# Weight row, output chunks and a third place for the last unit's turned banks: a hand-planned hybrid attention layer

## The reference, cut to what matters

```
h = rmsnorm(x, norm_g)
q, k, v, g of groups A, B, C, and f_logit = split(h @ w_in)      # w_in: 1024 x 6152
A: stick-breaking attention  w[t,s] = sigmoid(z[t,s]) * prod_{s<r<t} sigmoid(-z[t,r]),  s < t
B: softmax over own chunk of 64 + 8 chunks before, q and k normed, clipped relative bias
C: softmax(z + cum_t - cum_s), s <= t, with cum = cumsum(log_sigmoid(f_logit + b)), q and k normed
mixed = concat(o_A*silu(g_A), o_B*silu(g_B), o_C*silu(g_C))       # 1024 x 1536
out = x + mixed @ w_out                                            # w_out: 1536 x 1024
```

## Time and profile before

| | us |
|---|---|
| median of 3 runs | 1028.04 (1027.76 to 1029.62) |
| profiled execution, its own time | 1033.86 |
| its span, first to last instruction | 1032.1 |
| PE busy in the span | 1002.9 (97%) |
| DVE busy | 701.9 (68%) |
| ACT busy | 630.7 (61%) |
| POOL busy | 127.6 (12%) |
| idle time of PE behind a DVE, ACT or DMA wait from 839 us to the end | 7.5 |

### The profile page before, as it was taken

The page is one execution under the profiler, slowest core; times in us unless marked ns, Lnnn a source line. Parts: engine busy times, 40 slices in busy tenths (PEclk is TensorE's granted clock), DMA queues, the critical chain, the costliest instruction groups (busy, mean ns, idle before and its releaser), DMA issues.

```text
span 1032.1 us, 16364 instructions
## 1 busy us (share of the span) xinstructions
PE 1002.9 (97%) x5688; PEld 913.1 (88%) x5688; DVE 701.9 (68%) x1418; ACT 630.7 (61%) x1230; POOL 127.6 (12%) x152
## 2 busy tenths in 40 slices
PE   6999999999999999999999999999999999898998
PEld 6989989899899998998998998998998997786887
DVE  4655675765856867767768659889789787886100
ACT  6658775766766867767767667556567565453000
POOL 1310211111202122112112201011011010000000
PEclk9999999999999999999999999999999999999999
DMA  8245152242431623414314304205214248622820
GB/s 254 84 127 132 29 144 60 76 121 55 120 98 31 158 58 82 123 48 112 100 50 121 85 22 112 73 22 126 58 37 116 62 108 237 209 92 82 335 98 35
DMA packets 118066, 105.51 MB, mean 102 GB/s; under 512 B 10048, under 2 KB 94024, under 8 KB 117984
## 3 DMA queue, kind: packets, MB, share of 16 engines
q1 hardware_dynamic: 115904, 104.43, 36.7%
q10 hardware_dynamic: 2080, 0.04, 0.1%
HBM read 62.44 MB, written 19.98 MB: 80 GB/s over the span
## 4 chain that ended last, share of the span: by engine, by line
PE 81%; DVE 9%; DMA 4%; ACT 3%; issue 2%; SPq 1%; POOL 0%; DVEq 0%; ACTq 0%; POOLq 0%
PE psP L1247 36%; PE psP L1251 9%; PE psO L1330 9%; PE psT L1312 8%; PE psS L1295 4%; PE psS L1296 4%; PE psP L1378 3%; PE psS L1378 3%; DVE rb L1151 2%; PE psO L1378 2%; PE psP L1348 2%; PE psT L1269 1%; DVE z L1154 1%; DMA wraw<-in_w_out_dram 1%; DMA wraw<-in_w_in_dram 1%
## 5 line engine op out<-in xcount | busy, mean ns | idle before, releaser
L1247 PE MATMUL psP<-big 128*128 128x384 f32 (+1 forms) x2304 | 476.1, 344 | 5.3 <-DVE big L1012 4.8
L1247 PEld LDWEIGHTS psP<-big 128*128 128x128 f32 x2304 | 397.1, 189 | 14.1 <-DVE big L1012 6.1
L1162 DVE TENSOR_TENSOR pt<-psT,pt 128x512 fp32r<-128x512 f32 (+1 forms) x224 | 143.5, 642 | 124.0 <-ACT pt L954 123.1
L954 ACT ACTIVATE pt<-psT 128x512 fp32r<-128x512 f32 (+1 forms) x224 | 124.9, 558 | 106.2 <-PE psT L1312 105.7
L1251 PE MATMUL psP<-big 128*128 128x512 f32 x576 | 155.9, 403 | 0.0
L1330 PE MATMUL psO<-pt,vst 128*128 128x512 f32 (+3 forms) x576 | 137.2, 338 | 6.8 <-DVE pt L1162 6.1
L1312 PE MATMUL psT<-identr,z 128*128 128x128 f32 x816 | 125.2, 272 | 0.0
L1251 PEld LDWEIGHTS psP<-big 128*128 128x128 f32 x576 | 102.3, 189 | 18.0
L1330 PEld LDWEIGHTS psO<-pt,vst 128*128 128x128 f32 x576 | 101.7, 189 | 18.6 <-issue 9.8
L1312 PEld LDWEIGHTS psT<-identr,z 128*128 128x128 f32 x816 | 102.7, 140 | 15.7
L1295 PE MATMUL psS<-stack 128*128 128x256 f32 (+3 forms) x288 | 97.0, 344 | 2.4 <-ACT z L930 1.8
(11 more groups left out here) (114 smaller groups left out, 1137.9 us busy)
## 6 DMA issues: line engine op xcount, KB each, us to landing
stack<-stack SPq DMA_DIRECT2D x192, 128.0 KB, 2.3
wraw<-in_w_in_dram SPq DMA_DIRECT2D x90, 192.0 KB, 2.7
wraw<-in_w_in_dram SPq DMA_DIRECT2D x24, 256.0 KB, 3.8
mixed_scratch<-mst SPq DMA_DIRECT2D x24, 256.0 KB, 2.6
mixed_scratch<-gate SPq DMA_DIRECT2D x24, 256.0 KB, 3.2
wraw<-in_w_out_dram SPq DMA_DIRECT2D x24, 256.0 KB, 3.2
rb<-decay_scratch SPq DMA_DIRECT2D x8, 512.0 KB, 4.2
big<-mixed_scratch SPq DMA_DIRECT2D x8, 512.0 KB, 5.9
```

The lines of the kernel that those rows point to most:

```text
L954: nc.scalar.activation(pt[:, ci % PTR, 0, 0:w], psT[:, m % NT, 0:w], ACT.Copy).then_inc(s_hi, 1)
L1162: nc.vector.tensor_tensor(pt[:, ci % PTR, 1, 0:w], psT[:, m % NT, 0:w], pt[:, ci % PTR, 0, 0:w].bitcast(F32), ALU.subtract).then_inc(s_eva ...
L1247: ins = nc.tensor.matmul(dst[:, 0:TOKW - first], hT[a][:, k, i * P:(i + 1) * P], wpair[b][:, k, first:TOKW], start=(k == 0 and q == 0), st ...
```

## The change

Four tables of due times, and the last unit's banks.

- Row 7 of the next pair's weights is split at 3.6 and not at 4.05 in pairs 8, 9 and 10; pairs 4 to 7 keep 4.05.
- Chunks 8 to 15 of `w_out` come at 5.0 to 8.15 and not at 4.6 to 7.05 (chunk 7 at 4.3 and not 4.25).
- The loads for token tiles 2 and 3 come at 5.2 and 8.0 and not at 4.3 and 7.0; the residual of the second half at 7.2 and not 7.7.
- In unit 47 the values of a bank are two turns behind, and its third bank has a place of its own: the 128 x 1024 of `stack` that held the queries of the last head. Each place is then free three banks later.

```diff
-BEHIND_TURN = {('weights', 2): 1.5, ('weights', 3): 1.9, ('weights', 4): 2.3, ('weights', 7): 4.05}
+BEHIND_TURN = {('weights', 2): 1.5, ('weights', 3): 1.9, ('weights', 4): 2.3}
+BEHIND_LAST = {('weights', 7): 4.05}
 KEYS_AT = 0.05
-WOUT = [round(0.6 + 0.6 * c, 2) for c in range(SOON)] + [round(3.9 + 0.35 * c, 2) for c in range(EARLY - SOON)]
+WOUT = [round(0.6 + 0.6 * c, 2) for c in range(SOON)] + [3.9, 4.3] + [round(5.0 + 0.45 * c, 2) for c in range(EARLY - MF)]
 FIRST_AT = 3.2
-MIXF = [1.1, 2.9, 4.3, 7.0]
-RESIDUAL = [0.3, 7.7, 9.7]
+MIXF = [1.1, 2.9, 5.2, 8.0]
+RESIDUAL = [0.3, 7.2, 9.7]
...
-        ahead = NEXT if j < PPG else {**NEXT, **BEHIND_TURN}
+        ahead = NEXT if j < PPG else {**NEXT, **BEHIND_TURN, **(BEHIND_LAST if j < NORMED else {})}
...
 def turned_steps(u):
-    seq = [("turn", u, 0)]
-    for b in range(1, len(banks(u))):
-        seq += [("turn", u, b), ("values", u, b - 1)]
-    return seq + [("values", u, len(banks(u)) - 1)]
+    nb, ahead = len(banks(u)), 2 if u == UNITS - 1 else 1
+    seq = [("turn", u, b) for b in range(ahead)]
+    for b in range(ahead, nb):
+        seq += [("turn", u, b), ("values", u, b - ahead)]
+    return seq + [("values", u, b) for b in range(nb - ahead, nb)]
...
+THIRD = VAL0[UNITS - 1]
+def bank_place(ci):
+    b = ci - THIRD
+    if b < 0:
+        return ci % PTR, ci - PTR + 1
+    if b < PTR:
+        return ci % PTR, ci - PTR + 1
+    if b == PTR:
+        return PTR, 0
+    return bank_place(ci - PTR - 1)[0], ci - PTR
...
+        ptv = [pt[:, i, :, :] for i in range(PTR)] + [stack[:, 1, 0, :].rearrange("p (v c) -> p v c", v=2)]
...
-                    if ci >= PTR:
-                        act.wait_ge(s_pv, ci - PTR + 1)
+                    place, behind = bank_place(ci)
+                    if behind > 0:
+                        act.wait_ge(s_pv, behind)
+                    if place == PTR:
+                        act.wait_ge(s_scores, NB)
```

More of the change, by code:

```diff
@@ L950, in _ @@
                     w = P * sum(c for _, _, c in banks(u)[b])
-                    if ci >= PTR:
-                        act.wait_ge(s_pv, ci - PTR + 1)
+                    place, behind = bank_place(ci)
[3 more added lines that the diff above has]
+                        act.wait_ge(s_scores, NB)
                     act.wait_ge(s_turn, m + 1)
-                    nc.scalar.activation(pt[:, ci % PTR, 0, 0:w], psT[:, m % NT, 0:w], ACT.Copy).then_inc(s_hi, 1)
+                    nc.scalar.activation(ptv[place][:, 0, 0:w], psT[:, m % NT, 0:w], ACT.Copy).then_inc(s_hi, 1)
                 if kind == "gather":
@@ L1160, in _ @@
                     w = P * sum(c for _, _, c in banks(u)[b])
+                    place = ptv[bank_place(ci)[0]]
                     dve.wait_ge(s_hi, m + 1)
-                    nc.vector.tensor_tensor(pt[:, ci % PTR, 1, 0:w], psT[:, m % NT, 0:w],
-                                            pt[:, ci % PTR, 0, 0:w].bitcast(F32), ALU.subtract).then_inc(s_evac, 1)
+                    nc.vector.tensor_tensor(place[:, 1, 0:w], psT[:, m % NT, 0:w],
+                                            place[:, 0, 0:w].bitcast(F32), ALU.subtract).then_inc(s_evac, 1)
                 if kind == "gather":
@@ L1330, in _ @@
                             ins = nc.tensor.matmul(psO[:, q0 * P:(q0 + cnt) * P], vst[:, (2 * j + s) % 3, kb, :],
-                                                   pt[:, ci % PTR, v, col:col + cnt * P], start=(b == 0 and v == 0),
+                                                   ptv[bank_place(ci)[0]][:, v, col:col + cnt * P], start=(b == 0 and v == 0),
                                                    stop=(b == nb - 1 and v == 1 and pi == len(pieces) - 1))
```

## The result

| | before | after |
|---|---|---|
| median of 12 runs each, us | 1027.9 (1026.5 to 1030.8) | 1031.3 (1028.9 to 1034.2) |
| ratio | | 1.0031 (1.0021 to 1.0041) |
| profiled execution, its own time | 1033.9 | 1030.4 |
| its span | 1032.1 | 1028.6 |
| PE busy | 1002.9 | 1000.8 |

The change makes the kernel 3.2 us slower (0.31%); 3.2 us faster was forecast, with 1020.5 to 1028.2 us as the range, and "slower" had a chance of 0.09. Yet the two profiled executions say 3.5 us faster. The one of before was unusual: 1033.9 us, above all twelve timed runs (at most 1030.8).

The account below looks back on a forecast made before the run. PE, busy 1002.9 of 1032.1 us, was taken as the bound, so only its idle and slow-clock time could be won. Terms -3.45 + 0.2 + 0 = -3.2 us took the median 1028.04 to 1024.8 us, range 1020.5 to 1028.2.

Parts of the forecast that it names:

- Row 7: Pairs 8 to 10, first projection's second half: an earlier split removes three PE waits totalling 3.75 us, winning 3.45 us.
- Its chunk was asked for three steps before: Row 7's split at 3.6: its load was requested three steps earlier, by row 4's step.
- at most 0.61 - 0.56 = 0.05 us: Row 7's 0.61 us DVE instruction between sixth and seventh turned bank, where DVE idles 0.56 us: cost at most 0.05 us.
- Row 7 wins nothing: Rival, chance 0.12: DVE is full for 25 us behind row 7's new place, so waits only move; 1028.2 us.
- The third place: Unit 47: three bank waits, 2.0 us together, go, but the mixed rows' wait grows to 2.8 us or more; worth 0.
- clock -1.7 to +1.7, 0 taken: End of kernel, third place: clock effect between -1.7 and +1.7 us, counted as 0.
- I keep 1.7 us of loss as before: Around tile 2's first product: a 3.4 us idle stretch replaces one of 1.80 us, with the 1.7 us clock loss unchanged.
- My rival of a halved clock: Rival, chance 0.08: tile 2's wait reaches 5.6 us and brings two more slow stretches, 3.4 us; +2.4, 1030.4 us.
- The tables: Output chunks, tile loads, residual: new 3.4 us wait less 1.80 and 1.44 us, +0.2 us (-1.6 to +2.4).
- the wait for tile 2: First product of token tile 2: its later load makes PE wait 3.4 us (1.6 to 5.6).
- the waits of 1.80 and 1.44 us: Pair 11: PE's waits before a score step (for ACT) and a values step (for DVE) both go.
- That tile 2's data can't pass chunk 11's: Tile 2's load: ring order keeps it behind chunk 11's 256 KB, fitting the upper half of landing times.

Follow-up runs that it names:

- experiment 2: Only weight row 7's split moved to 3.6 in pairs 8 to 10, against the kernel before; ratio 0.9997 (0.9985 to 1.0010).
- experiment 7: Weight row 7 split at 3.78, behind the last turned bank, in pairs 8 to 10, against the kernel before; ratio 0.9969 (0.9957 to 0.9981).
- experiment 4: Only the last unit's third bank place, with values two turns behind, against the kernel before; ratio 1.0027 (1.0013 to 1.0041).
- experiment 1: The kernel before, unchanged, run and profiled again; ratio 1.0000 (0.9986 to 1.0015), profiled span 1025.9 us.
- experiment 5: The last unit's third place alone plus ten useless PE matmuls behind the last values, against the kernel before; ratio 1.0004 (0.9993 to 1.0015).
- experiment 12: The whole change plus 24 useless PE matmuls, 14 before tile 2's first product and 10 behind the last values, against the kernel before; ratio 0.9978.

## Why the prediction was wrong

The parts alone measure -0.3 + 0.7 + 2.8 = +3.2 us, as the whole does. Each has an interval of about 1.3 us either way, so that they meet to the tenth is luck. Against the forecast terms -3.45, +0.2 and 0 the miss of 6.4 us is 3.15 in row 7, 0.5 in the tables and 2.8 in the third place. So two steps failed, each enough to spoil the forecast.

**Row 7** (taken at -3.45, is -0.3, interval -1.5 to +1.0). The step "Its chunk was asked for three steps before", so that its split costs "at most 0.61 - 0.56 = 0.05 us", failed. I took the chunk for landed without a row that showed it. In the profile after its load was issued at 630.32, only 1.9 us before ACT came to the split at 3.6, and took 3.52 us; ACT stood 1.6 to 2.0 us in the three pairs and held up the bank behind. PE's waits there sum to 2.27 us where 3.75 stood: 1.5 us won on paper, not 3.45. Of these the time shows 0.3; the mean clock of experiment 2 was lower than that of before by what 0.7 us of time are, which twelve runs can hardly tell from nothing. At 3.78, behind that bank, the forecast's sum comes true: 3.2 us (experiment 7). My rival "Row 7 wins nothing" had the right size, but looked for the cause in DVE's full stretch and not in ACT and a DMA.

**The third place** (taken at 0, is +2.8). Its waits did as said: 2.0 us for banks went but for 0.2, one wait for the mixed rows of 2.8 us or more was forecast and 3.03 measured, and PE did not resume sooner. The step that failed is "clock -1.7 to +1.7, 0 taken". I took the idle time to cost the clock the same in one piece as in four (0.94, 0.44, 0.65 and 0.78 us with work between them). With one piece of 2.68 us every run of experiment 4 had 0.998 or less, and filling the piece took the loss away.

**The base.** Behind this lies that I took the clock losses of the earlier trace rows as terms of before ("I keep 1.7 us of loss as before"). They were chance of one execution; experiment 1 has none. Beside the experiments 32 of 88 runs of before had 0.998 or less. Of the change all twelve had 0.997 or less, and seven 0.994 or 0.995, one stretch more than its profile shows. In clock it is 0.9958 for the change and 0.9989 to 0.9995 for before, 3 to 4 us. Taking 1.03 us for each 0.001 out of every run leaves, as an estimate and in the mean, 1027.1 us for the change and 1027.4 to 1028.1 for before on the four chips: the shorter waits are worth 0.4 to 1.0 us, and the clock costs more. My rival of a halved clock had the right mechanism, but I asked for two more stretches of it in one place and gave it 0.08.

**The tables** (taken at +0.2, is +0.7, interval -0.6 to +2.1). Right in place and mechanism: the wait for tile 2 was forecast at 3.4 us (1.6 to 5.6) and is 4.07; the waits of 1.80 and 1.44 us went. The two loads were issued at 868.10, 3.3 us before PE wanted them, where 3.1 was forecast, and took longer to land than the median I had used. That tile 2's data can't pass chunk 11's is shown by no run, and no term rests on it.

The Trainium skill, "TensorE: Matmul & The Clock Gate", section "HAM oscillation", advises for matmuls of small M to do all the work on one tile before waiting for DMA, so that PE keeps its fast clock. That waits for DMA cost the clock, experiments 4, 5 and 12 agree, with 2.2 to 4 us for one or two waits of 2.7 to 4.1 us.

## What to carry to other kernels

Where PE is 97% busy, don't gather its short idle pieces into one before a fixed landing: here the sum of the waits stayed, and the clock was lost on top. Look at the granted clock of several executions before a slow stretch enters a sum, and compare the profiled execution's time with the median first. Before a split is moved ahead of something, look when its load is issued and when it lands, and what else the engine that reads it first has behind it.

## What the runs showed of the hardware that I had not expected

Ten useless matmuls (2.45 us) in a gap that would be idle made the kernel some 2.4 us faster than the same kernel without them.

The fourteen profiled executions together show which idle pieces of PE, from 60 us on, were followed by a lower clock:

| one idle piece of PE, us | pieces | clock low right behind it |
|---|---|---|
| 1.00 to 1.52 | 38 | 0 |
| 1.80 to 2.30 | 8 | 6 |
| 2.68 to 4.62 | 5 | 5 |

A low clock followed pieces that a DMA, ACT and DVE ended; those of 2.68 us and more all ended with a DMA. Between 1.80 and 2.30 us the length alone doesn't decide: 1.81 and 1.83 us left the clock at 1.00, 1.80 and 1.89 didn't. Nor is one long piece needed: the slow stretch at 948 us in the first profile of before stands behind four pieces of 0.94, 0.44, 0.65 and 0.78 us, and in experiment 1 the first three without the fourth left it at 1.00. What decides there, these runs leave open. The first wait of the program, 7.5 us, was followed by 1.00 in all fourteen.
